# A decoder trunk with gathered experts: an accumulator handed over half by half, and a route stage moved five slots

## What is computed

```python
def peer_ffn(h, w_q, sub_keys, expert_u, expert_v):        # for each block of 128 positions
    q = einsum('nd,de->ne', xb, w_q)                       # 8 heads, two half keys of 128 each
    s = einsum('nhie,ike->nhik', q, keys)
    top_s, top_i = lax.top_k(s, 16)                        # twice 16 of 128
    cand_s = top_s[..., 0, :, None] + top_s[..., 1, None, :]
    best_s, best_pos = lax.top_k(cand_s, 16)               # 16 of the pairs
    idx = ...                                              # expert number, of 128*128
    gate = softmax(best_s)
    act = gelu(einsum('nhkd,nd->nhk', expert_u[idx], xb))
    return einsum('nhk,nhkd->nd', gate * act, expert_v[idx])
```

## Time and profile before

| | us |
|---|---|
| median of three runs (lowest, highest) | 1641.92 (1640.35, 1643.54) |
| the profiled execution, device time | 1642.93 |
| its span in the trace | 1641.1 |
| share of the span: DVE, PE busy | 72%, 73% |
| moved by DMA | 665.99 MB, mean 406 GB/s |

### The profile page before, as it was taken

How to read it: one execution, slowest core, us unless ns; L and a number is a source line. 1 busy time by engine, 2 the same in 40 slices (tenths; PEclk the granted TensorE clock), 3 DMA queues, 4 the chain that set the end, 5 groups by cost and what they waited for, 6 DMA issues and landing times.

```text
span 1641.1 us, 21546 instructions
## 1 busy us (share of the span) xinstructions
PE 1191.8 (73%) x7384; PEld 579.4 (35%) x7384; DVE 1174.9 (72%) x3348; ACT 522.6 (32%) x1207; POOL 590.9 (36%) x525
## 2 busy tenths in 40 slices
PE   8876685768748885978785798599597955555555
PEld 3552232225405662432263366344134611111111
DVE  3557868776678778897665877689966577777755
ACT  0132134222223563642132256355211322222211
POOL 1043333534433223323333432232343444444451
PEclk9987898989968997998998799799798977787776
DMA  9599999999999999999999999999999999999996
GB/s 378 245 375 422 423 423 421 421 422 422 422 412 382 422 423 409 397 422 424 420 423 422 400 422 423 423 403 402 366 412 423 421 421 421 421 421 421 421 421 263
DMA packets 84076, 665.99 MB, mean 406 GB/s; under 512 B 9376, under 2 KB 9520, under 8 KB 10752
## 3 DMA queue, kind: packets, MB, share of 16 engines
q0 software_dynamic: 74608, 540.65, 79.8%
q1 hardware_dynamic: 9216, 123.46, 17.9%
q10 hardware_dynamic: 144, 0.52, 0.1%
HBM read 663.55 MB, written 1.05 MB: 405 GB/s over the span
## 4 chain that ended last, share of the span: by engine, by line
DMA 30%; PE 28%; DVE 26%; ACT 7%; issue 7%; POOL 2%; DVEq 0%; POOLq 0%; ACTq 0%; SPq 0%
DMA ring<-in_experts,idx 30%; PE acc L846 11%; DVE ring L1453 9%; PE act_bank L551 6%; PE dve_bank L537 6%; DVE scratch L1097 3%; ACT L884 2%; DVE onehot L1097 2%; POOL ring L480 2%; ACT scratch L884 2%; ACT diag L1031 1%; DVE scratch L1269 1%; PE act_bank L537 1%; ACT scratch L958 1%; PE act_bank L773 1%
## 5 line engine op out<-in xcount | busy, mean ns | idle before, releaser
L480 POOL DMA_INDIRECT ring<-in_experts,idx x512 | 584.9, 1142 | 1005.3 <-PE acc L846 789.8
L846 PE MATMUL acc<-ring,diag 64*64 64x512 f32 x4096 | 617.8, 731 | 362.3 <-ACT diag L1031 340.6
L1453 DVE CUSTOM_DVE_ANT_0 ring<-ring,hn 128x1024 f32<-128x1024 f32 x512 | 622.4, 1224 | 267.3 <-DMA ring<-in_experts,idx 247.8
L846 PEld LDWEIGHTS acc<-ring,diag 64*64 64x64 f32 x4096 | 155.6, 154 | 723.3 <-ACT diag L1031 468.1
L1024 ACT ACTIVATE acts<-dots 128x2 f32<-128x2 f32 x256 | 52.0, 203 | 720.9 <-DVE dots L1453 703.0
L551 PE MATMUL act_bank<-hnT,wbuf 128*128 128x128 f32 x1856 | 235.3, 285 | 24.9 <-ACT scratch L958 17.4
L551 PEld LDWEIGHTS act_bank<-hnT,wbuf 128*128 128x128 f32 x1856 | 221.8, 198 | 76.3 <-issue 76.3
L1031 ACT ACTIVATE diag<-cst,coefs 128x64 f32<-128x64 f32 x512 | 150.2, 340 | 226.1 <-DVE coefs L1461 191.7
L884 ACT ACT_TABLE_LOAD x80 | 102.6, 1283 | 19.2 <-DMA rowc<-in_rows 16.9
L1461 DVE TENSOR_TENSOR coefs<-acts,gate 128x2 f32<-128x2 f32 x256 | 41.3, 161 | 74.4 <-ACT acts L1024 54.7
L1024 ACT ACT_TABLE_LOAD x68 | 87.2, 1283 | 5.9 <-ACT scratch L884 0.4
(11 more groups left out here) (143 smaller groups left out, 911.2 us busy)
## 6 DMA issues: line engine op xcount, KB each, us to landing
wbuf<-in_weights SPq DMA_DIRECT2D x50, 2048.0 KB
ring<-in_weights SPq DMA_DIRECT2D x5, 2048.0 KB, 19.8
ring<-in_experts,idx POOLq DMA_INDIRECT x512
kept<-in_weights SPq DMA_DIRECT2D x2, 2048.0 KB, 23.6
wbuf<-in_weights SPq DMA_DIRECT2D x2, 1024.0 KB, 7.5
scratch<-in_bias POOLq DMA_DIRECT2D x1, 1024.0 KB, 11.5
scratch<-in_bands POOLq DMA_DIRECT2D x1, 768.0 KB, 13.4
h<-in_x SPq DMA_DIRECT2D x1, 512.0 KB, 4.2
```

The costliest lines, as they stand in the source:

```text
L480: pool.indirect_dma_start(ring[:, n % RING], None, io[f"experts{layer}"], bass.IndirectOffsetOnAxis(idx[:, at:at + 1], 0),).then_inc(sem(f ...
L846: last[rows] = pe.matmul(acc[rows][half][home:home + HALF_P], diag[part, n % DIAGS], ring[part, slot, D + half * CW:D + (half + 1) * CW], ...
L1453: dve.tensor_tensor_reduce(out=ring[:, slot, 0:D], in0=ring[:, slot, 0:D], in1=hn[:, phase % NBLK], scale=1.0, scalar=0.0, op0=ALU.mult, o ...
```

## The change

Three edits go together. In `ROUTE_DUE` head 1 of the phases 1 to 3 is due five slots sooner, at -9, -6, -3 and 0. ACT and DVE tell `odd_copied` and `acc_read` once for each half of the columns instead of once for both. And PE waits for half 0 ahead of the first pair's matmuls into the banks of half 0, and for half 1 ahead of the others.

```diff
+            if _head == 1 and _phase:
+                _due -= 5
+            ROUTE_DUE.append(max(_due, _part) if _head and not _phase else _due)
...
                 for half in range(2):
+                    if start and g:
+                        pe.wait_ge(sem("acc_read"), 2 * (g // STEPS - 1) + half + 1)
+                        pe.wait_ge(sem("odd_copied"), 2 * (g // STEPS - 1) + half + 1)
                     for odd in range(GROUP):
...
                 for n in range(SLOTS + GROUP):
-                    if n == GROUP and phase:
-                        pe.wait_ge(sem("acc_read"), phase)
-                        pe.wait_ge(sem("odd_copied"), phase)
...
-                lane.after(started)
-                lane.tell("odd_copied")
+                    lane.after(started)
+                    lane.tell("odd_copied")
...
-                lane.after(started)
-                lane.tell("acc_read")
+                    lane.after(started)
+                    lane.tell("acc_read")
 
             def add_odd(phase):
 
+                lane.need("odd_copied")
                 lane.need("odd_copied")
```

More of the change, by code:

```diff
@@ L138 @@
                 _due = _phase * SLOTS - 17 + 1.5 * _part
-            ROUTE_DUE.append(max(_due, _part) if _head else _due)
+            if _head == 1 and _phase:
+                _due -= 5
+            ROUTE_DUE.append(max(_due, _part) if _head and not _phase else _due)
 C_ID, C_TRI, C_STRI, C_IOTA = 0, P, 2 * P, 3 * P
```

## The result

| | device us, median (lowest to highest) | executions |
|---|---|---|
| before | 1643.2 (1639.72 to 1648.53) | 19 |
| changed | 1645.96 (1642.62 to 1648.32) | 19 |

The ratio is 1.0017, with a 95% interval from 1.001 to 1.0024. The change costs 2.8 us (1.6 to 3.9 by the interval). That is under the 0.2% that I had called the least to be told, but 19 executions of each tell it apart from nothing, and 1645.96 lies outside my range of 1636.5 to 1643.2. The profiled execution of the changed kernel took 1643.91 us, its span 1642.1 us.

A forecast was written before the change was run, and what follows sets the result against it. The prediction took DMA to bound the kernel: -1.2 us at the first turn, 0 at the second and third, 0 for hidden added waits, giving 1640.7 us against the median 1641.92; range 1636.5 to 1643.2 us.

The forecast's parts named there:

- the least to be told: Whole kernel: a measurement can tell about 0.2%, 3.3 us, from no change, so the forecast counted as "same".
- The dot of slot 3: First turn, DVE: with head 1's part 2 moved ahead of the turn, this dot comes 3.9 us sooner.
- PE's first pair: First turn: with the hand-over by halves PE starts and finishes this pair 1.4 us sooner.
- the gather of slot 14: First turn: comes some 4.4 us sooner against the dot of slot 2, before the DMA rate collapses.
- the dips at both turns: DMA falls to 387 and 242 GB/s behind the first turn, 349 behind the second; no window should stay below 380.
- The added wait: Inside `add_even` and ACT's copies: 0.05 us, bounds 0 and 0.4 us a turn, hidden behind 4.5 us gained on DVE.
- The rival of the bytes won back in full: First and second turn: the dips are worth 4.8 + 1.9 = 6.7 us, giving 1635.2 us; chance 0.18.
- The rule of the Trainium skill that I went by: DMA engines finish independently and only the full count of 16 means landed; completion spacing gives 1.2 us, not 4.8.
- the first turn lost 74.3 - 73.1 = 1.2 us: First turn, slot 2 to 27: 74.3 us against 29 undisturbed row sets at 2.522 us; 1.2 us to be won back.
- What happens in the middle of the phases is not touched [...] and what comes later only shifts.: Mid-phase: DVE waits for DMA again at 548.94 and 971.86, so it had caught up; no time change there.
- The third rival: End of a phase: sooner routing delays next-phase gathers, 3.9 us a turn, 11.7 us in all, 1653.6 us; chance 0.07.

The follow-up runs named there:

- two copies of before: The unchanged kernel before, profiled two more times, one execution each (`c1_before`, `c2_before`): 1642.19 and 1645.79 us.
- the second copy: `c2_before`: the kernel before, unchanged, run once more for its profile; 1645.79 us in a single execution.
- e3_hold42: Changed kernel, with SyncE holding phase 1's slot 42 weight chunk until the pair of slots 42 and 43 is summed; 1642.82 us, ratio 0.9999 to before.
- f2_hold42: Changed kernel with the slot 42 chunk held until pair 42 and 43 is summed, repeated on the changed kernel's chip; 1642.75 us, ratio 0.9996 to before.

## Why the prediction was wrong

**Right: the turn's mechanics.** The dot of slot 3 came 3.6 us sooner against the dot of slot 2 (forecast 3.9), PE's first pair 1.4 (forecast 1.4), the gather of slot 14 5.0 (forecast 4.4), the dips at both turns went. The added wait was 0.11 us, within 0 to 0.4, and 0.11 or 0.12 us at each turn in every profile with the halves (2.94 to 2.95 us against 2.83), so not nothing. The rival of the bytes won back in full fell: the dips of 6.7 us by bytes went, and the time did not follow (from slot 2 to 27 of the first turn the gathers' queue moved 26.4 MB instead of 25.0). By the trace's semaphore events the first and the last of the 16 engines came through the set of slot 27 3.7 and 5.7 us apart in the two copies of before, and 9.3 to 10.8 us apart in the three profiles of the changed kernel; at slot 47 it was at most 6.1 us in the two profiles of before with the early order, 9.0 in the one with the late order, and 11.2 to 11.8 in the changed kernel. I read this so that the dips' bytes went into the lead of engines that were ahead anyway; no run tests that reading. The rule of the Trainium skill that I went by (DMA: Bandwidth & Descriptors, "Why a DMA increments its semaphore by 16 and not by 1") held in this: the dot of slot 42 in the changed kernel started 0.02 us behind the sixteenth increment and 9.9 us behind the first.

**Mis-sized: "the first turn lost 74.3 - 73.1 = 1.2 us".** By the same distance, slot 2 to slot 27, the kernel before took 74.30, 74.15 and 72.88 us in three profiles, and the changed one 73.73, 73.82 and 73.77. The mean of before is 73.8. I read a loss out of one execution that three do not bear out. The gain at the first turn is 0 us within 0.5. The measure itself was at fault: I took the distance between two dots released by DMA for a fixed price for each row set, with the weights counted alike. But the second copy's 72.88 us are followed by 58.66 from slot 27 to 42, against 57.55 and 57.77, and the second turn has the same exchange between the two kernels (see the result). From slot 2 to slot 42 the three profiles of before took 131.5 to 131.9 us and those of the changed kernel 131.5 to 131.6: about 0.2 us gained at the first turn, and nothing at the second (131.5 to 131.7 in both).

**The step that failed: "What happens in the middle of the phases is not touched [...] and what comes later only shifts."** DVE did catch up with DMA at slots 27 and 42, and I took that for a point behind which the past is forgotten. The row sets do shift as one there, but the weight chunks are asked for by PE's progress, not by DMA's. In the changed kernel PE frees a chunk's place sooner against the same row set: in the first profiles three earlier chunks are asked for 58.4, 44.5 and 32.8 us ahead of slot 42's dot instead of 56.3, 42.5 and 30.7, and the one in question 10.7 us behind it instead of 12.2 or 12.7. The smaller backlog is the likely reason, but not the only way there: the second copy of before has the late order with the old backlog and the old three times. The chunk then shares DMA with the sets of slots 43 to 47, and the last of these releases 78.3 us of DVE's own work. Moving that one request by 2 us and nothing else took the loss away (`e3_hold42`, `f2_hold42`). The Trainium skill (DMA: Bandwidth & Descriptors, "Queues, rings and completion order") states that an engine takes turns between the queues for which it has work; the 44.3% and 40.3% of DMA that the weights queue had in that stretch, beside the gathers' queue, agree with that, though no row here shows the turns themselves.

**What the change really does to the time.** It does not make a slow path that was not there. Before falls to the late order too, in one of three profiles. The changed kernel did in three of three, the route edit alone in one of one, the halves alone in one of one. The two profiles of before with the chunk held tell a little more, since the chunk ahead of it was free: it was asked for 0.5 and 1.0 us behind the dot of slot 42, as in the early order (0.3 and 0.8), and not 0.9 to 3.1 us ahead of it, as in all six profiles with the late order. By these, before takes the late order in one of five. Of the three profiles of the changed kernel with this chunk held, two had the chunk ahead of it as in the late order (3.1 and 3.2 us ahead) and one in between (0.3). 2.4 us for two thirds to four fifths more of the executions is 1.6 to 1.9 us, an estimate; the measured cost is 1.6 to 3.9 us in the first comparison and -0.2 to 2.8 us (0.9999 to 1.0017) in the last. That the order explains the larger part is shown by the holds. How often each kernel takes which order rests on few profiles, what tips an execution into one of them stays open, and why the halves alone had the late order in their one profile stays open: it could be chance.

**The third rival**, a hole ahead of the turn by the sooner routing, did not come: from the dot of slot 118 to that of slot 2 the kernel before took 35.62 us at the first turn and the changed one 35.66. At the second turn it is 44.8 to 45.1 us in all three profiles of each, and at the third 34.0 to 35.8 before and 34.9 to 35.1 in the changed kernel.

## What to carry to other kernels

A kernel bound by DMA can lose time with every DMA engine busy: look at which transfer the waiting engine needs next, and what shares the DMA engines with it. When a backlog is cut, list the requests that are paced by the engine that is now sooner, weights above all, and follow them to the next place where one transfer releases a long stretch of an engine's own work. Small gains read as a difference of two stretches in one profile want a second profile first.

## What the runs showed that I had not expected

One request decides 2.4 to 3.2 us of 1643, and within 1.2 us of its own time: asked for 11.0 us after slot 42's dot or less it costs all of it, at 12.2 us most of it is gone. The kernel before with that chunk held back had the lowest medians of all experiments (1642.2 and 1641.95 us); against before that is a ratio of 0.9988 (0.9978 to 0.9998) in the first comparison and 0.9994 (0.9985 to 1.0002) in the second, on the same chip, so a gain of 1 to 2 us that the second comparison alone does not establish.

Phase 2 has the late order always. In all 14 profiles, held or not, before or changed, its slots 42 to 47 take 22.3 us, and DVE waits 2.2 to 4.5 us for the set of slot 47, after which the dot of slot 68 follows in 74.6 to 74.8 us every time. The same 2 to 3 us may be lost there in both kernels. No run holds that phase's chunk, so this is not shown.
